# Order and tiles of the two halves of the first mixer: gated linear attention ahead of the recurrence

## The chip, the cores and the metric

The kernel runs on one core of one Trainium2 chip. The metric is the device time of one execution in microseconds (us). The kernel before takes 2805.81 us, the median of three runs (2805.32 to 2807.16).

## What is computed

Two blocks of two layers each on x (512 tokens, width 1024). The change lies in the first mixer of the first block; everything behind it stays. Cut to what matters:

```python
def even_mixer(u, w_in, conv_w, conv_b, rg_wa, rg_ba, rg_wx, rg_bx, rg_lam,
               gla_w_up, gla_b_up, gla_norm_g, w_out):
    xr, yr, q, k, v, g, zl = split(u @ w_in, [512, 512, 256, 256, 512, 512, 16])
    # recurrent half
    x = causal_dwconv(xr, conv_w, conv_b)
    r, i = sigmoid(x @ rg_wa + rg_ba), sigmoid(x @ rg_wx + rg_bx)      # 8 blocks of 64
    log_a = 8 * r * log_sigmoid(rg_lam)
    h = scan(exp(log_a), sqrt(-expm1(2 * log_a)) * (i * x))            # h_t = a_t h_(t-1) + u_t
    rg_out = h * gelu(yr)
    # gated linear attention (GLA), 4 heads, chunks of 64 tokens
    log_alpha = log_sigmoid(zl @ gla_w_up + gla_b_up) / 16
    bcum = cumsum(log_alpha) within a chunk
    q_dec, k_dec, k_end = q*exp(bcum), k*exp(-bcum), k*exp(b_last - bcum)
    o = causal(q_dec k_dec^T) v + q_dec state;  state = decay * state + k_end^T v
    o = rms_norm(o, gla_norm_g) * silu(g)
    return concat([rg_out, o]) @ w_out
```

## The kernel before

**Layout.** Activations lie transposed, 128 features in the partitions and 512 tokens along the free axis, so a vector of 1024 features is 8 tiles of 128x512. `H` ("hidden") has 32 such tiles, `M` ("mixer_out") 8, `TMP` ("tmp") 2, and `B` is the 8 PSUM banks. The mixer's tiles in `H` are named by number on the lines that begin with `XR, YR, Q, K_, GG, VT` (L448 to L451). The names EB, QD, KD, KE and T1 of GLA lie on tiles 20 to 29, the same tiles as RT, IT and AT_ of the recurrence (20 to 31). So GLA's elementwise work can't begin before the recurrence is through with them; `gla_u` waits for `rg_scan` 3.

**Products.** Every weight product is in fp32 split in two parts: weights high and low, input high and low, three matmuls for each 128x128 block. A product of one output tile (`gemm`, L654 to L656) is 24 matmuls of 128x128 on 512 columns. `gemm_tok` makes v with the tokens in the partitions, in 4 panels of 24 matmuls (L715 to L717). `gemm_pair` makes two outputs, the second two k-tiles behind the first, so that inputs which are just being made can be taken in as they come (L697 to L699). Its `busy` (L625) are matmuls of constants whose result isn't used. `gemm_bank` hands out banks 1 and 0 in turn, and waits for the eviction of the product before last.

**Weights.** A stream of 512 KB panels is loaded by SyncE into a ring of 4. Most panels are weights: ScalarE (ACT) writes the high part (`high`, L2047), VectorE (DVE) the low part (`low`, L1296), into one of 3 places. The others ("ada") belong to the modulations: VectorE alone multiplies and sums them (`modulation`, L1305). Their order in the stream is fixed: v0, v1, ada, v2, ada, v3, yr0, ada, yr1, ada, yr2, yr3, ada, gg0, ada, gg1, gg2, ada, gg3, ada, and then each of the eight even_out panels with two ada panels behind it. VectorE frees the place in the ring. `prepare(ahead(key))` stands by hand at places of the ScalarE and VectorE programs: it makes the panels up to the second one behind `key`. `high` waits until the third panel back has been used.

**Order.** Each engine's program is written out by hand, in order, and an engine that waits holds up all behind it. The functions `even` of the three programs hold the mixer. Before the change:

- TensorE (PE): eight products at once (`gemm_eight`), zl, v0 to v3 with the gate matmuls of the recurrence (L818) ahead of v2 and v3, GLA's logits 0 (L824), yr0, logits 1, yr1, yr2, yr3, the transposes of k_end (L835), gg0, GLA's scores and k^T v (L844, L853), gg1, gg2, GLA's outputs 0 (L870, L877), gg3, outputs 1, the sums of `gla_norm` (L890), then the pair even_out 0 and 1 with the second `gla_norm` inside it, then even_out 2 to 7.
- VectorE: convolution (L1332), the recurrence (L1542 to L1555), GLA's decays (`softplus_neg`, L1562 to L1578), mask and state (L1586, L1594), gelu (L1599 to L1605), then GLA's norm and gates (L1611 to L1624). `input_low` (L1463) splits the eight results.
- ScalarE: sigmoids (L2203), exp and tanh (L2208, L2212), sqrt (L2217), the eviction of v (L2068), softplus of GLA (L2225 and L2081 to L2085), its exps (L2231, L2238), evictions of yr and gg (L2061), gelu's square and tanh, the GLA outputs (L2257, L2262), the roots (L2089, L2092) and `input_high` (L2072), which writes UHI, the tiles that the gg products read.

Where ScalarE needs a function that its active table doesn't hold, a table load stands ahead of it (ACT_TABLE_LOAD). `exp_ln_tables` loads one by hand, which holds both exp and ln.

## Time and profile before

| | before |
|---|---|
| median of three runs | 2805.81 us |
| the profiled execution | 2809.87 us |
| its span (first to last instruction) | 2808.4 us |
| mean granted TensorE clock | 0.993 |
| TensorE busy | 2694.2 us, 96% |
| VectorE busy | 1626.6 us, 58% |
| ScalarE busy | 1122.9 us, 40% |
| DMA | 336.42 MB, mean 120 GB/s |

A row of an engine's timeline has the start and the length in us, the engine, the line in the kernel, the operation, its tiles written and read, and how often it stands in a row; in brackets the idle time ahead of it and who ended it. Matmuls are pipelined, so the time from one start to the next is what one costs, not its length. A row of "waits" has who waited, for whom, and then the total in us, how often, and the longest. A row of "windows" has the stretch in us, and for each engine its busy time and its number of instructions, and behind them the granted clock (1.00 is 2.4 GHz, 0.50 is 1.2 GHz), the busy share of the DMA engines, and GB/s.

### The profile page before, as it was taken

Reading aid. Unit: us, or ns where it says so; the run is one execution under the profiler, and the core shown is the slowest. Engines: PE = TensorE matmul, PEld = TensorE weight load, DVE = VectorE, ACT = ScalarE, POOL = GpSimd, SP = SyncE. Lnnn points to the kernel's source line nnn. Section 1 sums busy time; section 2 is a strip of 40 time slices with the busy share of each in tenths; the row PEclk is TensorE's granted clock in tenths of the full one; section 3 lists DMA queues with packets and bytes.
Section 4 is the critical chain, followed back from the end, with each engine's and each line's share of the span. In section 5 each row is a group of like instructions: output and inputs, shape, how many; then the busy total and the mean of one; then the engine's idle time right before and its main releaser. Section 6 shows DMA issues by size and latency. Waiting matters only on the chain.

```text
span 2808.4 us, 41819 instructions
## 1 busy us (share of the span) xinstructions
PE 2694.2 (96%) x17268; PEld 2119.8 (75%) x17268; DVE 1626.6 (58%) x2919; ACT 1122.9 (40%) x1964; POOL 9.4 (0%) x21
## 2 busy tenths in 40 slices
PE   7899999999999999999998899999999988999998
PEld 6677888867666788886876667888878766788886
DVE  7678646573555874657456755443465577533334
ACT  3544324234555432423345653222334466422222
POOL 0000000000000000000000000000000000000000
PEclk9999999999999999999999999999999999999999
DMA  8344555532221365563330013444433200222322
GB/s 308 105 150 166 195 173 180 179 133 91 76 76 56 117 206 198 181 205 111 103 116 17 3 61 120 143 142 150 143 120 108 90 3 2 92 96 98 98 98 83
DMA packets 92094, 336.42 MB, mean 120 GB/s; under 512 B 10481, under 2 KB 10737, under 8 KB 91777
## 3 DMA queue, kind: packets, MB, share of 16 engines
q1 hardware_dynamic: 86656, 314.87, 33.8%
q10 hardware_dynamic: 3936, 14.64, 1.4%
q0 software_dynamic: 1312, 4.23, 0.5%
q8 instruction: 138, 2.26, 0.3%
q14 instruction: 52, 0.42, 0.0%
HBM read 331.57 MB, written 2.13 MB: 119 GB/s over the span
## 4 chain that ended last, share of the span: by engine, by line
PE 46%; DVE 3%; ACT 3%; issue 1%; DVEq 0%; ACTq 0%
PE bank L654 12%; PE bank L655 12%; PE bank L656 12%; PE bank L933 1%; ACT probs L2294 1%; PE bank L918 1%; PE bank L904 1%; PE bank L1018 1%; PE bank L697 0%; PE bank L698 0%; PE bank L699 0%; PE bank L991 0%; PE bank L1192 0%; PE bank L1124 0%; PE bank L1006 0%
## 5 line engine op out<-in xcount | busy, mean ns | idle before, releaser
L1296 DVE TENSOR_TENSOR weights_low<-weight_ring,weights_high 128x1024 fp32r<-128x1024 f32 x404 | 493.9, 1224 | 428.0 <-ACT weights_high L2047 427.9
L654 PE MATMUL bank<-in_high,weights_high 128*128 128x512 f32 x1816 | 718.2, 396 | 15.0 <-DVE weights_low L1296 9.9
L656 PE MATMUL bank<-in_high,weights_low 128*128 128x512 f32 x1816 | 708.2, 390 | 0.0
L655 PE MATMUL bank<-in_low,weights_high 128*128 128x512 f32 x1816 | 708.0, 390 | 0.0
L2047 ACT ACTIVATE weights_high<-weight_ring 128x1024 fp32r<-128x1024 f32 x404 | 424.5, 1051 | 432.2 <-PE bank L656 301.4
L654 PEld LDWEIGHTS bank<-in_high,weights_high 128*128 128x128 f32 x1816 | 341.6, 188 | 100.1 <-issue 17.8
L655 PEld LDWEIGHTS bank<-in_low,weights_high 128*128 128x128 f32 x1816 | 341.8, 188 | 72.4 <-issue 3.1
L656 PEld LDWEIGHTS bank<-in_high,weights_low 128*128 128x128 f32 x1816 | 341.4, 188 | 72.0
L654 PE MATMUL bank<-hidden_split,weights_high 128*128 128x512 f32 x864 | 336.9, 390 | 0.0
L656 PE MATMUL bank<-hidden_split,weights_low 128*128 128x512 f32 x864 | 336.1, 389 | 0.0
L655 PE MATMUL bank<-hidden_split,weights_high 128*128 128x512 f32 x864 | 336.1, 389 | 0.0
L1305 DVE CUSTOM_DVE_ANT_0 weight_ring<-weight_ring,silu_c,vectors 128x1024 f32<-128x1024 f32 x192 | 244.2, 1278 | 0.1
L655 PEld LDWEIGHTS bank<-hidden_split,weights_high 128*128 128x128 f32 x864 | 162.2, 188 | 34.1 <-issue 0.5
L654 PEld LDWEIGHTS bank<-hidden_split,weights_high 128*128 128x128 f32 x864 | 162.2, 188 | 34.1 <-issue 0.5
L656 PEld LDWEIGHTS bank<-hidden_split,weights_low 128*128 128x128 f32 x864 | 162.2, 188 | 33.8
L2162 ACT ACTIVATE hidden_split<-tmp 128x512 fp32r<-128x512 f32 x108 | 68.3, 632 | 269.3 <-DVE tmp L1836 200.7
L2061 ACT ACTIVATE tmp<-bank 128x512 f32<-128x512 f32 x76 | 45.4, 597 | 228.7 <-PE bank L656 225.1
L1468 DVE TENSOR_TENSOR hidden_split<-tmp,hidden_split 128x512 fp32r<-128x512 f32 x108 | 74.8, 692 | 75.4 <-ACT hidden_split L2162 75.4
L1357 DVE SCALAR_TENSOR_TENSOR residual<-bank,modulations,residual 128x512 f32<-128x512 f32 x64 | 48.0, 750 | 118.7 <-PE bank L656 118.7
L2294 ACT ACTIVATE probs<-probs,columns 128x256 f32<-128x256 f32 (+4 forms) x144 | 73.7, 514 | 101.8 <-DVE columns L1641 100.0
L1836 DVE TENSOR_TENSOR tmp<-bank,tmp 128x512 f32<-128x512 f32 x44 | 30.4, 691 | 113.6 <-PE bank L656 113.6
L2061 ACT ACTIVATE tmp<-bank,vectors 128x512 f32<-128x512 f32 (+1 forms) x65 | 44.6, 687 | 129.0 <-PE bank L656 125.8
(394 smaller groups left out, 3377.6 us busy)
## 6 DMA issues: line engine op xcount, KB each, us to landing
weight_ring<-stream SPq DMA_DIRECT2D x596, 512.0 KB, 3.4
mixer_out<-cmp ACTq DMA_DIRECT2D x6, 1024.0 KB, 4.9
hidden<-forget_rows POOLq DMA_DIRECT2D x16, 256.0 KB, 3.6
residual<-x ACTq DMA_DIRECT2D x4, 512.0 KB, 8.4
mixer_out<-cmp SPq DMA_DIRECT2D x2, 1024.0 KB, 6.3
out<-mixer_out ACTq DMA_DIRECT2D x4, 512.0 KB, 3.0
constants<-consts ACTq DMA_DIRECT2D x1, 1821.5 KB, 9.9
silu_c<-c ACTq DMA_DIRECT2D x2, 512.0 KB, 4.4
```

Source lines behind the costliest of these rows:

```text
L654: pe.matmul(bank[:, :], WHI[:, z, cols], high, start=(k == 0), stop=False)
L655: pe.matmul(bank[:, :], WHI[:, z, cols], low, start=False, stop=False)
L656: ins = pe.matmul(bank[:, :], WLO[:, z, cols], high, start=False, stop=(k == ktiles - 1))
L1296: v.tensor_tensor(WLO[:, z, :], ring[:, n % RING, :], WHI[:, z, :].bitcast(F32), ALU.subtract).then_inc(*mark("weights_low", "low", n))
L1305: v.tensor_tensor_reduce(w, w, SC[:, :], 1.0, vec1("ada_b", col, col + 1), ALU.mult, ALU.add, MODS[:, col:col + 1]).then_inc(*mark("modula ...
L1357: v.scalar_tensor_tensor(X[:, m, :], B_of(key)[:, :], gcol_[:, m:m + 1], X[:, m, :], ALU.mult, ALU.add).then_inc(*mark("residual", "evicte ...
L1468: v.tensor_tensor(HSPLIT[:, 1, at_, :], tmp, HSPLIT[:, 0, at_, :].bitcast(F32), ALU.subtract).then_inc(*mark("vector_mlp", *event))
L1836: v.tensor_tensor(tmp, B_of(("gup", l, j))[:, :], tmp, ALU.mult).then_inc(*mark("vector_mlp", "evicted", ("gup", l, j)))
L2047: s.activation(WHI[:, i % NSPLIT, :], ring[:, n % RING, :], ACT.Copy).then_inc(*mark("weights_high", "high", n))
L2061: s.activation(dst, view(B_of(key)[:, :]), func, **kw).then_inc(*mark("scalar_evict", "evicted", key))
L2162: s.activation(HSPLIT[:, 0, at_, :], tmp, ACT.Copy).then_inc(*mark("scalar_mlp", *event))
L2294: s.activation(p, p, ACT.Exp, bias=nm, scale=-1.0, accum_out=COL[:, c + 2 + z:c + 3 + z]).then_inc(*mark(sem, *name, "exp", i))
```

## The change

It reorders the first mixer and moves tiles; no product and no elementwise operation on data is left out, and the stream of weights keeps its order.

- **Tiles.** GLA's softplus and k_dec go to TMP, its cumulated decays to M 6 and 7, a temporary to M 4 and 5, EB to H 14 and 15; q_dec and k_end are written over q and k. None of them lies on a tile of the recurrence any more. The recurrence's own temporary leaves M 4 to 7 for RT.
- **Order.** The logits go ahead of v1; softplus and decays go ahead of the recurrence, between and around its sigmoids. The transposes of k_end go behind v3, scores and k^T v behind yr0, then yr1, yr2, yr3. The four gg products now stand behind the parts of GLA that make its output: outputs 0, gg0, outputs 1, gg1, norm 0, gg2, norm 1, gg3.
- **Split.** The four recurrent results of the mixer are split into other tiles (H 4 to 7, where yr was, and H 0 to 3), not into UHI and ULO, which the gg products still read. The pair of even_out has no `busy` and no norm inside it.
- **Tables.** With the new order ScalarE's functions alternate more often between tables.

```diff
     XR, YR, Q, K_, GG, VT = 0, 4, 8, 10, 12, 16
     RT, IT, AT_ = 20, 24, 28
-    EB, QD, KD, KE, T1, KET = 20, 22, 24, 26, 28, 30
-    OG = [Q, Q + 1, K_, K_ + 1]
+    KET, EB = 12, 14
+    OG = [K_, K_ + 1, Q, Q + 1]
+    gla_x = lambda m: TMP[:, m, 0:T]
+    gla_cum = lambda m: M[:, 6 + m, :]
+    gla_t = lambda m: M[:, 4 + m, :]
+    MIX_LO = (2, 3, 0, 1)
+    even_split = lambda k: (HSPLIT[:, 0, YR + k, :], HSPLIT[:, 0, MIX_LO[k], :]) if k < 4 else u_split(k)
...
@@ TensorE, even()
+                elif i == 1:
+                    for m in range(2):
+                        pe.wait_ge(*at("evicted", ("q", m)))
+                        pe.wait_ge(*at("evicted", ("zl",)))
+                        ins = pe.matmul(B[2 + m][:, :], vec1("gla_up", m * P, m * P + P, rows=16), ZL, start=True, stop=True)
+                        ins.then_inc(*mark("tensor_even", "gla_logits", m))
...
             gemm_tok(("v",), 4, 2, 512, ("v",), B[4:8], gates)
+            pe.wait_ge(*at("loads"))
             for m in range(2):
-                pe.wait_ge(*at("rg_gate", 1, 3))
...
-                gemm(("yr", m), u_split)
-            gemm(("yr", 2), u_split)
-            gemm(("yr", 3), u_split)
-            for m in range(2):
+                pe.wait_ge(*at("rg_gate", 1, 3 * m))
                 pe.wait_ge(*at("gla_ke", m))
...
-            gemm(("gg", 0), u_split)
+            gemm(("yr", 0), u_split)
+            pe.wait_ge(*at("v_out", NTB - 1))
             pe.wait_ge(*at("ket", 1))
...
-            gemm(("gg", 1), u_split)
-            gemm(("gg", 2), u_split)
+            for m in range(1, 4):
+                gemm(("yr", m), u_split)
...
             pe.wait_ge(*at("gla_state"))
             gla_out(0)
+            gemm(("gg", 0), u_split)
+            gla_out(1)
+            gemm(("gg", 1), u_split)
+            gla_norm(0)
+            gemm(("gg", 2), u_split)
+            gla_norm(1)
             gemm(("gg", 3), u_split)
-            gla_out(1)
-            gla_norm(0)
...
-        gemm_pair([("even_out", 0), ("even_out", 1)], u_split, lambda k: ("even_low", k),
-                  lambda k: gla_norm(1) if k == 3 else None)
-        project(lambda m: ("even_out", m), 0, None, 2)
+        gemm_pair([("even_out", 0), ("even_out", 1)], even_split, lambda k: ("even_low", k), idle=0)
+        project(lambda m: ("even_out", m), 0, None, 2, even_split)
@@ VectorE, even()
...
+            for m in range(2):
+                softplus_neg(sem, gla_x(m), gla_x(m), gla_cum(m), ("gla", m))
+            for m in range(2):
+                v.tensor_scalar(gla_x(m), gla_x(m), -1.0 / 16.0, None, ALU.mult).then_inc(*step(sem))
+                v.wait_ge(*last(sem))
+                v.tensor_tensor_scan(gla_cum(m), const("chunk_reset"), gla_x(m), 0.0, ALU.mult, ALU.add).then_inc(
+                    *mark(sem, "gla_cum", m))
+            prepare(ahead(("v", 2)))
+            for m in range(2):
+                qd, k_, kd, bc, eb, t1 = H[:, Q + m, :], H[:, K_ + m, :], gla_x(m), gla_cum(m), H[:, EB + m, :], gla_t(m)
+                v.wait_ge(*at("gla_exp", m))
+                v.tensor_tensor(qd, qd, eb, ALU.mult).then_inc(*step(sem))
+                v.tensor_tensor(kd, k_, t1, ALU.mult).then_inc(*step(sem))
...
+                v.tensor_tensor(t3, bc3[:, :, GLA_CH - 1:GLA_CH].broadcast_to([P, 8, GLA_CH]), bc3,
+                                ALU.subtract).then_inc(*mark(sem, "gla_end", m))
+            for m in range(2):
+                k_ = H[:, K_ + m, :]
+                v.wait_ge(*at("gla_end_exp", m))
+                v.tensor_tensor(k_, k_, gla_t(m), ALU.mult).then_inc(*mark(sem, "gla_ke", m))
+            prepare(ahead(("v", 3)))
...
             v.tensor_tensor(i_, i_, xr, ALU.mult).then_inc(*step(sem))
...
             v.wait_ge(*at("rg_decay"))
...
+            v.tensor_tensor(xr, a, a, ALU.mult).then_inc(*step(sem))
...
+            v.scalar_tensor_tensor(r, xr, 1.0, r, ALU.add, ALU.mult).then_inc(*mark(sem, "rg_ratio"))
+            prepare(ahead(("yr", 0)))
+            v.wait_ge(*at("rg_ratio"))
+            v.memset(H[:, XR:XR + 2, :], 0.0).then_inc(*step(sem))
             v.wait_ge(*at("rg_sqrt"))
...
+            v.tensor_tensor(i_, i_, r, ALU.mult).then_inc(*mark(sem, "rg_in"))
...
             for m in range(4):
+                if m == 2:
+                    prepare(ahead(("yr", 1)))
                 v.tensor_tensor_scan(M[:, m, :], H[:, AT_ + m, :], H[:, IT + m, :], 0.0, ALU.mult, ALU.add).then_inc(
                     *mark(sem, "rg_scan", m))
...
+            prepare(ahead(("yr", 2)))
...
+            prepare(ahead(("yr", 3)))
...
+            prepare(ahead(("gg", 0)))
...
+            def mix_low(k):
+                high, lo = even_split(k)
+                v.wait_ge(*at("even_high", k))
+                v.tensor_tensor(lo, M[:, k, :], high.bitcast(F32), ALU.subtract).then_inc(*mark(sem, "even_low", k))
...
+                v.wait_ge(*at("evicted", ("gg", h)))
...
+            gla_sum(0)
+            v.wait_ge(*at("yr_tanh"))
+            v.scalar_tensor_tensor(th, th, 1.0, yr, ALU.add, ALU.mult).then_inc(*step(sem))
+            v.wait_ge(*last(sem))
+            v.scalar_tensor_tensor(rgo, th, 0.5, rgo, ALU.mult, ALU.mult).then_inc(*mark(sem, "rg_mix"))
+            prepare(ahead(("gg", 1)))
+            mix_low(0)
+            mix_low(1)
+            gla_sum(1)
+            mix_low(2)
+            mix_low(3)
+            prepare(ahead(("gg", 2)))
+            gla_mix(0)
+            gla_mix(1)
+            gla_mix(2)
+            prepare(ahead(("gg", 3)))
+            mix_low(4)
+            gla_mix(3)
+            for h in range(1, 4):
+                mix_low(4 + h)
@@ ScalarE, even()
...
             evict(("zl",), ZL, view=lambda z: z[0:16, :])
+            s.wait_ge(*at("loads"))
+            s.wait_ge(*at("xr_conv", 1))
             prepare(ahead(("v", 1)))
...
+            for m in range(2):
+                s.wait_ge(*at("gla_logits", m))
+                s.activation(gla_x(m), B[2 + m][:, :], ACT.Identity, bias=vec1("gla_b", m, m + 1)).then_inc(*mark(sem, "gla_u", m))
+            for m in range(2):
+                s.wait_ge(*at("gla_u", m))
+                softplus(sem, gla_x(m), gla_cum(m), ("gla", m))
...
+            gate(0)
+            prepare(ahead(("v", 2)))
+            for m in range(2):
+                s.wait_ge(*at("gla_cum", m))
+                s.activation(H[:, EB + m, :], gla_cum(m), ACT.Exp).then_inc(*step(sem))
+                s.activation(gla_t(m), gla_cum(m), ACT.Exp, scale=-1.0).then_inc(*mark(sem, "gla_exp", m))
+            for m in range(2):
+                s.wait_ge(*at("gla_end", m))
+                s.activation(gla_t(m), gla_t(m), ACT.Exp).then_inc(*mark(sem, "gla_end_exp", m))
+            prepare(ahead(("v", 3)))
+            gate(1)
...
             for m in range(4):
...
             for m in range(4):
...
+                ins = s.activation(H[:, RT + m, :], H[:, RT + m, :], ACT.Tanh, scale=LS[:, m:m + 1])
...
             for m in range(2):
                 s.wait_ge(*at("ke_turned", m))
...
+                s.activation(ket[:, :, m * P:m * P + P], r4(B[2 + m][:, :]), ACT.Copy).then_inc(*mark(sem, "ket", m))
+            prepare(ahead(("yr", 0)))
+            s.wait_ge(*at("rg_ratio"))
+            s.activation(wide(RT), wide(RT), ACT.Sqrt, scale=-1.0).then_inc(*mark(sem, "rg_sqrt"))
+            for m in range(4):
+                evict(("yr", m), H[:, YR + m, :])
+            th = M[:, 4:8, :].rearrange("p a t -> p (a t)")
+            s.wait_ge(*at("gla_ke", 1))
             s.wait_ge(*at("evicted", ("yr", 3)))
...
             s.activation(th, wide(YR), ACT.Square).then_inc(*mark(sem, "yr_square"))
...
+            prepare(ahead(("gg", 0)))
             intra(0)
+            s.wait_ge(*at("yr_poly"))
+            s.activation(th, th, ACT.Tanh, scale=float(np.sqrt(2.0 / np.pi))).then_inc(*mark(sem, "yr_tanh"))
             square(0)
+            evict(("gg", 0), H[:, GG, :], ACT.Silu)
+            prepare(ahead(("gg", 1)))
+            mix_high(0, ("rg_mix",))
+            mix_high(1, ("rg_mix",))
+            intra(1)
+            mix_high(2, ("rg_mix",))
+            mix_high(3, ("rg_mix",))
+            s.wait_ge(*at("gla_state"))
+            evict(("gg", 1), H[:, GG + 1, :], ACT.Silu)
+            square(1)
+            prepare(ahead(("gg", 2)))
+            exp_ln_tables()
+            for h in range(4):
+                root(h)
+            evict(("gg", 2), H[:, GG + 2, :], ACT.Silu)
             evict(("gg", 3), H[:, GG + 3, :], ACT.Silu)
...
+            for h in range(4):
+                mix_high(4 + h, ("gla_mix", h))
             exp_ln_tables()
```

Of the hunks of VectorE and ScalarE only the new order is shown; the order that it replaces is that of the functions printed above. `gate(half)` is the loop over `rg_gate`, `mix_high` is `input_high` with the new place for its result, and `root`, `square` and `intra` are as before.

## Rows read from the trace of the kernel before

**Rows 1.** The page, part 1: busy time, share of the span, instructions.

```profile
PE 2694.2 (96%) x17268; PEld 2119.8 (75%) x17268; DVE 1626.6 (58%) x2919; ACT 1122.9 (40%) x1964; POOL 9.4 (0%) x21
```

**Rows 2.** The waits of TensorE between 60 and 230 us.

```profile
PE bank L654 <- DVE weights_low L1296: 8.7, 4, 7.6
PE bank L835 <- DVE hidden L1578: 2.7, 1, 2.7
PE bank L890 <- ACT hidden L2262: 2.3, 1, 2.3
...
PE bank L697 <- DVE in_low L1463: 1.6, 3, 0.9
```

**Rows 3.** The waits of ScalarE between 60 and 230 us, the first.

```profile
ACT weights_high L2047 <- DMA weight_ring<-stream: 28.3, 8, 5.7
```

**Rows 4.** The timeline of TensorE, from the first v panel to even_out 2 and 3.

```profile
68.50 0.39 PE L715 MATMUL bank<-weights_high,in_high 128*128 128x512 f32 x1
...
79.38 3.59 PE L818 MATMUL bank<-hidden 128*128 128x512 f32 x8
...
97.24 1.12 PE L824 MATMUL bank<-probs_T,vectors 16*128 16x512 f32 x2
...
119.00 0.76 PE L654 MATMUL bank<-in_high,weights_high 128*128 128x512 f32 x1 [7.55 <-DVE weights_low L1296]
119.56 0.63 PE L655 MATMUL bank<-in_low,weights_high 128*128 128x512 f32 x1
...
122.12 0.40 PE L655 MATMUL bank<-in_low,weights_high 128*128 128x512 f32 x1
...
134.90 0.66 PE L835 MATMUL bank<-constants,hidden 128*128 128x128 f32 x4 [2.66 <-DVE hidden L1578]
...
142.54 1.39 PE L844 MATMUL bank<-hidden 64*64 64x64 f32 x58
...
168.43 3.39 PE L625 MATMUL bank<-constants 128*128 128x384 f32 x10
...
178.06 1.99 PE L890 MATMUL bank<-hidden,constants 128*128 128x512 f32 x4 [2.30 <-ACT hidden L2262]
...
189.82 0.47 PE L654 MATMUL bank<-in_high,weights_high 128*128 128x512 f32 x1
...
195.83 0.47 PE L654 MATMUL bank<-in_high,weights_high 128*128 128x512 f32 x1 [0.30 <-DVE weights_low L1296]
```

**Rows 5.** Two windows of 4 us, around the longest wait and around a wait of 2.30 us.

```profile
116.00:120.00 4.00, 1.00 (x3) 0.84 (x4) 3.56 (x6) 3.90 (x7) 0.00 (x0) 0.50 0.32 91
...
176.00:180.00 4.00, 1.94 (x5) 0.99 (x6) 2.76 (x4) 3.94 (x7) 0.00 (x0) 1.00 0.00 0
```

**Rows 6.** The timeline of ScalarE, 92 to 176 us.

```profile
92.60 1.28 ACT L2208 ACT_TABLE_LOAD   x1
93.89 2.56 ACT L2208 ACTIVATE hidden<-hidden,columns 128x512 f32<-128x512 f32 x4
...
103.30 1.92 ACT L2217 ACTIVATE mixer_out<-mixer_out 128x2048 f32<-128x2048 f32 x1 [1.19 <-DVE mixer_out L1549]
105.12 2.04 ACT L2068 ACTIVATE hidden<-bank 128x512 f32<-128x512 f32 x4
...
175.69 0.71 ACT L2089 ACTIVATE hidden<-bank,constants 128x512 f32<-128x512 f32 x1
```

**Rows 7.** The timeline of VectorE, 92 to 153 us.

```profile
92.61 2.29 DVE L1542 TENSOR_TENSOR hidden<-hidden 128x2048 f32<-128x2048 f32 x1 [13.14 <-ACT hidden L2203]
...
107.85 4.57 DVE L1555 TENSOR_TENSOR_SCAN mixer_out<-hidden 128x512 f32<-128x512 f32 x4
...
116.42 1.28 DVE L1305 CUSTOM_DVE_ANT_0 weight_ring<-weight_ring,silu_c,vectors 128x1024 f32<-128x1024 f32 x1
...
117.63 1.22 DVE L1296 TENSOR_TENSOR weights_low<-weight_ring,weights_high 128x1024 fp32r<-128x1024 f32 x1
...
148.80 4.46 DVE L1594 SCALAR_TENSOR_TENSOR hidden<-hidden,bank 128x128 f32<-128x128 f32 x14
```

More of the change, by code:

```diff
@@ L776, in layer_norm, with project @@
             ins.then_inc(*mark("tensor_means", "ln_var", i))
-        def project(key, i, ready, first=0):
+        def project(key, i, ready, first=0, x=u_split):
             for m in range(first, KT):
@@ L783, in project @@
                 else:
-                    gemm(key(m), u_split, ready=ready if m == 0 else None)
+                    gemm(key(m), x, ready=ready if m == 0 else None)
                 if i and m == 4:
@@ L2216, in even @@
-            s.wait_ge(*at("rg_ratio"))
-            s.activation(th, th, ACT.Sqrt, scale=-1.0).then_inc(*mark(sem, "rg_sqrt"))
             evict_blocks(("v",), ("v", 3), B[4:8], lambda b: vt[:, b, :], 512, ("v_out",))
-            exp_ln_tables()
-            s.wait_ge(*at("loads"))
-            for m in range(2):
-                x = H[:, QD + m, :]
-                s.wait_ge(*at("gla_logits", m))
-                s.wait_ge(*at("rg_scan", 3))
-                s.activation(x, B[2 + m][:, :], ACT.Identity, bias=vec1("gla_b", m, m + 1)).then_inc(*mark(sem, "gla_u", m))
-                s.wait_ge(*last(sem))
-                softplus(sem, x, H[:, KE + m, :], ("gla", m))
-                evict(("yr", m), H[:, YR + m, :])
```

126 lines of the change are left out of this document (25 added, 101 removed).

## The prediction, made before the changed kernel ran

> **What bounds the kernel now.** I read the busy times first: TensorE works 96% of the span [rows 1], so a gain has to be a wait of TensorE that goes, and there are few. Its waits between 60 and 230 us come next [rows 2], then its timeline, which gives the places [rows 4]. All of the change lies between the first v panel (68.50 us) and the start of even_out 2 (189.82 us): 121.3 us. Four things in it are not matmuls that the result needs:
> - Waits. Of the 8.7 us for weights_low, 7.55 stand ahead of yr2 at 119.00; 0.30 (at 195.83) and one more like it lie behind the stage, which leaves 8.0 inside. 2.7 are for GLA's k_end at 134.90, 2.3 for the ScalarE square of GLA's output at 178.06, 1.6 for input splits in the pair. Together 14.6 us. The reader should see that 7.55 us are not really for weights. VectorE and ScalarE come to yr2's panel late, since softplus of GLA had to wait for the scans (107.85 plus 4.57 [rows 7]), whose tiles it overwrites.
> - The unused matmuls at 168.43: 3.4 us.
> - A slow clock behind the long waits. From 119.56 to 122.12 six steps take 0.427 us each; at the full clock 48 matmuls from 68.50 to 79.38 take 0.227 each. The window around it was granted 0.50, the lower of the two levels (1.2 of 2.4 GHz) [rows 5]. About 7 steps here and 8 behind the wait at 134.90 (the rows there look the same) cost 0.2 us each: 3.1 us.
> All three make 21.1 us, so 100.2 us are work. No matmul is added, none that is used is removed.
>
> **The change: the early part.** I follow the three engines with durations from the rows. One gemm is 24 x 0.227 = 5.44 us, 5.5 with the switch between kinds of matmuls. The chain on TensorE: v0 68.5 to 73.9; both logits 2.2 (1.12 each [rows 4]); v1 to 81.6; gates 3.5 (79.38, x8 in 3.59); v2 to 90.6; gates to 94.0; v3 to 99.5; transposes 1.0; yr0 to 106.1. Then it waits for ket 1.
>
> ScalarE: the logits are there at 75.2 and 76.3, the softplus steps (two additions of bias, then six dependent steps at 0.64 and a little [rows 6]) are done at 80.9, and it loads the sigmoid table in time for the gates, which TensorE paces to 85.8. From here ScalarE is the chain: weights high 1.0, table 1.3, two exps to 89.3; VectorE does six 512-wide products for both halves (about 0.65 each, a quarter of the 2.29 of a wide one plus its start [rows 7]) to 93.3; exp of the end 0.6, high of yr1 1.0, table 1.3, four sigmoids 2.4: 98.7. Table 1.3, eight exps and tanhs 5.0 (2.56 for four [rows 6]): 104.9. Eviction of v 2.0 (105.12 [rows 6]), ket 1.2: **108.1**. TensorE had been ready at 106.1: a new wait of 2.1 us, and behind ScalarE's queue lie yr evictions that nobody needs yet. The added waits for the constants and for `xr_conv` 1 cost nothing: the second convolution ends near 68.3, before ScalarE gets there.
>
> **The recurrence, now behind GLA.** VectorE: i*x after the gates at 98.7, then a*a after the decays (102.4) and the ratio, 2.25 us each [rows 7]: 107.3. An ada panel and yr2's low part (1.28 and 1.22 [rows 7], the low waits for ScalarE's high at 109.1): 110.4. Sqrt on ScalarE, 1.3 table and 1.9 [rows 6]: 112.3. Product 2.3, four scans 4.6, yr3's low 1.1, ada and gg0's low 2.5: 122.9. Mask and clearing about 1.6 (an estimate from the two short operations on 512 columns), state 4.5 (148.80 [rows 7]): **128.9**. TensorE: scores and k^T v 3.3 (1.39 for the scores [rows 4], the rest about 1.9), to 111.5, then three yr to 128.1. A new wait of 0.8 us for the state.
>
> **GLA's output behind the gg products.** TensorE goes from 129.0: outputs 2.0 each, norms 1.8 each (178.06 [rows 4]), four gg 22.6: it is done with gg3 at 159.3. Each of the steps between finds its partner early: outputs 1 needs the eviction of outputs 0 (132.6, TensorE comes at 136.7); norm 0 needs the square (138.1, comes at 144.4), with gelu's tanh ahead of it on ScalarE; norm 1 needs the second square (147.6, comes at 151.8). So the 2.3 us wait goes, and so do those for the splits of the pair: the recurrent quarter of the mixer's output is split by 148 us. What is late next: ScalarE's roots 2 and 3 (two steps of about 0.65 each, 0.71 for the first [rows 6]) end at 155.3, the silu table 1.3 and gg2 0.5 make 157.1, VectorE's product needs that, and behind the product stand two ada panels and the low part of even_out 1: 0.7 + 2.5 + 1.2 = 161.5. The pair asks for both low parts at its start. A new wait of **2.3 us** (161.6 against 159.3). The pair then takes 11 us without another wait, for the last splits (163 to 165 us) are there before its fifth k-tile at 165.7.
>
> **The sum.** Stage before 121.3 us, after 100.2 + 2.1 + 0.8 + 2.3 = 105.4: 15.9 us less, taken as 16. The placing above, step by step, ends the pair at 172.8 and gives 17.0; I take the smaller, since a placing leaves small starts out. Behind the pair nothing changes. The weight stream there is tight: ScalarE waited 28.3 us for panels [rows 3]. But TensorE hardly waited for it (0.30, twice), and the panels of even_out 2 are made at 169 while TensorE wants them at 172.8, where before they came in the same moment. So that part keeps its length or gives 0.7 us. Against its own time the changed kernel's span would be 2808.4 - 16 = 2792.4. The profiled execution took 2809.87, 4.1 above the median, so I take 16 from the median: 2805.81 - 16 = **2789.8 us**.
>
> **The tables.** Table loads in the mixer rise from 6 to 9 or 10 (whether tanh and silu share one after the sqrt no row shows; it stands where ScalarE has time). A load costs 1.28 us, and the exp behind it starts 0.01 us after its end (92.60, 93.89 [rows 6]). Three of them are in the chain to ket and one is in the chain to the pair; they are counted above. The Trainium skill speaks against this order (ScalarE: Activation LUTs, "Rules for kernel authors": do all functions of one table before switching), and "What ACT_TABLE_LOAD costs" gives 1283 ns for the load and about 1380 ns more for a drain. By that page the four loads on the two chains would add some 5.5 us. The trace agrees with the load and not with the drain: the load at 92.60 follows the sigmoids without a gap.
>
> **The rivals.**
> 1. *ScalarE's chains are longer than I sum them.* The mechanism: six alternations between the tables and three hand-overs to VectorE stand ahead of ket, and each can add its start. The pure sum has nothing for it. Were each of the four loads to hold its engine for twice its row, 4 x 1.3 = 5.2 us come back: 2795.0. For it: each of these steps starts only when the one before is done, and a queue that holds copies of weights between them has no way around. Against it: the load at 92.60 and the exps at 93.89 follow on each other without a hole [rows 6]. The page's drain would come out here too, at 2789.8 + 5.5 = 2795.3. Chance 0.15.
> 2. *The clock falls in the new waits.* Behind the wait at 134.90 (2.66 us) eight matmuls ran slow, behind the wait of 2.30 us at 178.06 none (granted 1.00 there [rows 5]). The new waits of 2.1 and 2.3 us lie by the second, and no unused matmuls cover the one ahead of the pair. Two falls cost 2 x 1.6 = 3.2 us: 2793.0. Chance 0.15.
> 3. *The weight stream gives the gain back.* The pair starts 17 us sooner, and the places of the ring come free by VectorE. Were each of the six gemms behind it to wait 0.33 us, as two did before: 2 us back, 2791.8. The six gemms need 18 panels in 33 us; the stream moved at that pace before. Chance 0.05.
> 4. *Slower: the clock stays low.* If the new order starves TensorE in short waits all through the stage, matmuls run at 0.427 and not 0.227. It decides from the point where more than 80 additional matmuls (16 us by 0.2) run slow, a quarter of the stage's 336; with all from the ket wait on (nine gemms, 216 matmuls) it costs 43 us: 2833. Against it: in every stretch with long products the clock was back after 4 us. Chance 0.03.
> 5. *Nothing comes of it,* as VectorE is the true bound: it would need 16 more us of waits for low parts. VectorE is busy 58% of the span [rows 1], none of its operations is added, and in my placing each low part is there before TensorE asks for it, but for even_out 1. Chance 0.04, at 2805.
>
> **How the numbers follow.** The forecast has 0.58: its own range is 2787 to 2792.5 (16 us with 17 and the 0.7 of the stream at the low end, a short wait or two at the high end). Its range, rivals 1, 2 and 3 together hold about 0.93, of which 2786 to 2798 keeps eight in ten and a little; the low end allows for new waits that don't come (all 5.2 gone would be 2784.6), the high end for rivals 1 and 2 together. A measurement of this kernel can tell about 0.2% (5.6 us) from no change. All but rivals 4 and 5 are beyond that: faster 0.93, the same 0.04, slower 0.03.
>
> **What would show it.** In the profile after: no wait of TensorE near 7 us ahead of yr2; in its place one of about 2 us ahead of the scores with ket as releaser, one under 1 us ahead of the first outputs, one of 2 to 3 us ahead of the pair for weights_low. Even_out 2 starts near 173 us. The granted clock is 1.00 in the whole stage. Wrong would be: waits in the yr or gg gemms for weights_low (my VectorE queue is then too short), a start of even_out 2 beyond 178 us (rival 1), steps of 0.427 (rival 2), or a distance from even_out 2 to the end of the span that isn't the 2618.6 us of before within 1 us (rival 3).

## The result and the profile after

The changed kernel takes 2789.45 us (median of four runs, 2787.22 to 2789.91), the kernel before 2806.48 us (four runs, 2805.32 to 2809.57): a ratio of 0.9936, with a 95% interval of 0.9919 to 0.9953. That is 17.0 us less, where 16 were forecast. The profiled execution took 2789.05 us.

Busy times first (page, part 1, with the line that gives the span), against [rows 1]:

```profile
span 2787.6 us, 41806 instructions
...
PE 2685.7 (96%) x17258; PEld 2120.1 (76%) x17258; DVE 1626.7 (58%) x2919; ACT 1127.6 (40%) x1968; POOL 9.4 (0%) x21
```

VectorE works as long as before, ScalarE 4.7 us longer and with four more instructions, which are four more table loads. TensorE is busy 8.5 us less, of which 3.4 are the ten unused matmuls that went; the other 12.3 us of the 20.8 between the two profiled spans are its idle time, so its waits come next. These are those between 60 and 215 us (total, times, longest), against [rows 2]:

```profile
PE bank L702 <- DVE weights_low L1299: 2.9, 1, 2.9
PE bank L845 <- ACT hidden L2257: 2.2, 1, 2.2
PE bank L659 <- ACT hidden L2218: 1.7, 1, 1.7
PE bank L756 <- ACT mixer_out L2152: 1.4, 1, 1.4
```

The 7.55 us ahead of yr2, the 2.66 for k_end and the 2.30 for the square are gone. Two waits have come in: ahead of the scores for ket (L2257), and ahead of the pair for even_out 1's low part (L1299). The third lies at 61.60, ahead of the stage, and the fourth at the layer norm, behind it; the kernel before has both. The timeline of TensorE gives the places, against [rows 4]:

```profile
67.17 0.39 PE L720 MATMUL bank<-weights_high,in_high 128*128 128x512 f32 x1
...
97.97 1.03 PE L836 MATMUL bank<-constants,hidden 128*128 128x128 f32 x8
...
106.62 1.61 PE L845 MATMUL bank<-hidden,tmp 64*64 64x64 f32 x56 [2.17 <-ACT hidden L2257]
...
111.48 0.50 PE L659 MATMUL bank<-in_high,weights_high 128*128 128x512 f32 x1
...
128.02 1.16 PE L870 MATMUL bank<-hidden 64*64 64x64 f32 x64
...
160.78 0.47 PE L702 MATMUL bank<-hidden_split,weights_high 128*128 128x512 f32 x1 [2.89 <-DVE weights_low L1299]
...
162.38 0.63 PE L702 MATMUL bank<-hidden_split,weights_high 128*128 128x512 f32 x1
162.81 0.63 PE L703 MATMUL bank<-hidden_split,weights_high 128*128 128x512 f32 x1
...
173.38 0.39 PE L659 MATMUL bank<-hidden_split,weights_high 128*128 128x512 f32 x1
```

The stage runs from the first v panel at 67.17 to even_out 2 at 173.38: 106.2 us, where it took 121.3. From 106.62 to yr1 at 111.48 the scores and k^T v take 4.86 us, and 3.24 before. Behind the second wait the steps are 0.43 us apart, nearly twice the full rate's 0.227. Two windows tell why (length, then busy time with counts of PE, PEld, DVE, ACT and POOL, the granted clock, the DMA share, GB/s):

```profile
108.00:112.00 4.00, 4.00 (x84) 3.79 (x77) 2.92 (x3) 3.99 (x4) 0.00 (x0) 0.64 0.82 257
...
160.00:164.00 4.00, 3.22 (x10) 2.65 (x11) 3.90 (x7) 1.44 (x3) 0.00 (x0) 0.76 0.88 271
```

Behind both waits the clock fell for some microseconds to the lower of its two levels, 1.2 GHz. Each fall cost 1.6 us here (1.4 to 1.7 in the profiles below): 4.86 against 3.24, and 12.60 for the pair against the 10.96 to 11.01 that it took in five profiles below where its clock stayed at 1.00.

**Where the 20.8 us between the two profiled spans are.** Ahead of the stage 1.3. In it 15.1. From even_out 2 to the first layer-norm matmul 1.75 (35.25 to 33.50 us). Next to it 0.2, and in the second block, whose code is the same, 2.4 (1509.26 to 1506.84 us). That last stretch ran between 1506.8 and 1510.2 us in the other profiles, so the 2.4 are scatter between executions. Stage and even_out make 16.85, near the 17.0 of the medians. The agreement is closer than one profile can promise: the repeat below has a stage 1.5 us shorter, as one of the two falls didn't come.

### The profile page after: what moved, and what is told of

The parts are those of the page before. It is cut to its first block, busy times and chain, and to the rows that moved or that the text cites. A ratio compares the mean times of both kernels' runs of the same rounds, so it can differ in the third digit from the quotient of the medians.

```text
span 2787.6 us, 41806 instructions
## 1 busy us (share of the span) xinstructions
PE 2685.7 (96%) x17258; PEld 2120.1 (76%) x17258; DVE 1626.7 (58%) x2919; ACT 1127.6 (40%) x1968; POOL 9.4 (0%) x21
## 4 chain that ended last, share of the span: by engine, by line
PE 46%; ACT 4%; DVE 3%; issue 1%; DVEq 0%; ACTq 0%
PE bank L659 12%; PE bank L661 12%; PE bank L660 12%; ACT probs L2325 1%; PE bank L937 1%; PE bank L922 1%; PE bank L1022 1%; PE bank L908 1%; PE bank L702 0%; PE bank L703 0%; PE bank L704 0%; PE bank L1196 0%; PE bank L995 0%; PE bank L1010 0%; PE bank L1206 0%
## 5 line engine op out<-in xcount | busy, mean ns | idle before, releaser
L1299 DVE TENSOR_TENSOR weights_low<-weight_ring,weights_high 128x1024 fp32r<-128x1024 f32 x404 | 493.8, 1223 | 417.2 <-ACT weights_high L2069 417.1
L659 PE MATMUL bank<-in_high,weights_high 128*128 128x512 f32 x1792 | 708.1, 395 | 6.0 <-DVE in_low L1448 3.1
L661 PE MATMUL bank<-in_high,weights_low 128*128 128x512 f32 x1792 | 698.0, 390 | 0.0
L660 PE MATMUL bank<-in_low,weights_high 128*128 128x512 f32 x1792 | 698.0, 389 | 0.0
L659 PE MATMUL bank<-hidden_split,weights_high 128*128 128x512 f32 x888 | 346.4, 390 | 0.0
L660 PE MATMUL bank<-hidden_split,weights_high 128*128 128x512 f32 x888 | 345.6, 389 | 0.0
L661 PE MATMUL bank<-hidden_split,weights_low 128*128 128x512 f32 x888 | 345.6, 389 | 0.0
L660 PEld LDWEIGHTS bank<-hidden_split,weights_high 128*128 128x128 f32 x888 | 166.7, 188 | 35.1 <-issue 0.5
L659 PEld LDWEIGHTS bank<-hidden_split,weights_high 128*128 128x128 f32 x888 | 166.7, 188 | 34.9 <-issue 0.5
```

The source lines that it names most:

```text
L659: pe.matmul(bank[:, :], WHI[:, z, cols], high, start=(k == 0), stop=False)
L660: pe.matmul(bank[:, :], WHI[:, z, cols], low, start=False, stop=False)
L661: ins = pe.matmul(bank[:, :], WLO[:, z, cols], high, start=False, stop=(k == ktiles - 1))
L1299: v.tensor_tensor(WLO[:, z, :], ring[:, n % RING, :], WHI[:, z, :].bitcast(F32), ALU.subtract).then_inc(*mark("weights_low", "low", n))
```

## The experiments

Every diff is against the changed kernel. I read each profile by the same distances: "the stage" is the first v panel to even_out 2, "even_out" is even_out 2 to the first layer-norm matmul. Where no number of runs is given, the time is that of one execution, and what counts is its profile.

**Does a table load cost more than its row?** One more load goes into ScalarE's chain to ket.

```diff
 def even():            # ScalarE, behind the loop over rg_tanh
+            exp_ln_tables()
             evict_blocks(("v",) ...
```

> The changed kernel with one more table load (1.28 us) on ScalarE, between the last tanh of the recurrence and the eviction of v. If ScalarE's queue sets the wait ahead of the scores, as I hold, that wait grows from 2.17 to 3.45 us and the start of the scores moves by 1.28 us. The start of the first GLA outputs moves by 1.3 us with it, for yr1 to yr3 follow without a break. If a table load also held the engine for a drain of 1.38 us, as the Trainium skill has it (ScalarE: Activation LUTs, What ACT_TABLE_LOAD costs), the wait would grow by 2.66 us. If VectorE or the transposes set the wait, it stays at 2.17 us.

Measured: 2793.59 us. The wait ahead of the scores grew from 2.17 to 3.64 us, by 1.47. The first two rows are ScalarE's timeline, the third is TensorE's:

```profile
103.82 1.28 ACT L2098 ACT_TABLE_LOAD   x1
105.11 2.07 ACT L2090 ACTIVATE hidden<-bank 128x512 f32<-128x512 f32 x4
...
108.30 1.39 PE L845 MATMUL bank<-hidden,tmp 64*64 64x64 f32 x58 [3.64 <-ACT hidden L2258]
```

The load takes 1.28 and the eviction behind it starts 0.01 us after its end. ScalarE's chain is what TensorE waits for, and a load costs its row and 0.2 us more. Of these 0.12 are an overlap that it ends: the last tanh has a length of 0.71 us, the eviction starts 0.61 behind its start in the changed kernel, and the load here 0.73 behind it. Rival 1's doubled loads would have made the growth 2.6 us, and the drain that the Trainium skill states (ScalarE: Activation LUTs, "What ACT_TABLE_LOAD costs") 2.66.

**Can the ket wait be hidden behind yr1?**

```diff
             gemm(("yr", 0), u_split)
+            gemm(("yr", 1), u_split)
             ...
-            for m in range(1, 4):
+            for m in range(2, 4):
```

> The changed kernel with TensorE's yr1 ahead of the scores and k^T v instead of behind them. The wait for ket 2.17 us goes, as yr1 fills it, and with it the slow clock in the scores (1.6 us). My theory: the first outputs then wait for the GLA state, whose chain over ScalarE and VectorE (ready near 127.0 us after the span's start) doesn't move: TensorE comes 3.8 us sooner, at 124.2, and waits about 2.8 us. So the first outputs start only 1.0 us sooner (127.0). Rival: the state hangs on TensorE (k^T v), then all 3.8 us are gained.

Measured: 2790.25 us. The wait ahead of the scores is gone and the scores run at full clock, but the state, which needs k^T v, now comes late:

```profile
127.69 0.52 PE L871 MATMUL bank<-hidden 64*64 64x64 f32 x20 [2.84 <-DVE hidden L1600]
```

From v0 to the first outputs it is 59.93 us, where it was 60.85: 0.9 less, of 3.8 (2.17 of wait, 1.6 of slow clock) that went at the scores. The wait moved from one hand-over to the next. The clock didn't fall behind the 2.84 us. A wait of 2.17 us is worth only what the next one leaves of it.

**Is the pair's wait the order of VectorE's queue?** The low part of even_out 1's panel goes ahead of the third product of GLA's mix, and its high part ahead of the last two roots.

```diff
             gla_mix(1)
-            gla_mix(2)
             prepare(ahead(("gg", 3)))          # VectorE: low part
+            gla_mix(2)
...
-            for h in range(4):
-                root(h)
+            root(0)
+            root(1)
+            prepare(ahead(("gg", 3)))          # ScalarE: high part
+            root(2)
+            root(3)
```

> The changed kernel with the panel of even_out 1 (ScalarE: behind the second root; VectorE: its two ada panels and the low part behind the second of GLA's last products) made before, not after, the third product, which waits for the silu table. If VectorE's queue behind that product sets the wait of 2.89 us ahead of the pair, as I hold, the low part is there at 157.5 and the wait falls under 1 us (the eviction of gg3 is what is left, 0.7); the slow clock behind it (8 steps, 1.6 us) may go with it: even_out 2 starts 2.2 to 3.8 us sooner, if no split in the pair comes late. Rival: the stream's panel is not there before 156 us, then the wait stays over 2 us.

Measured: 2784.43 us, a stage of 101.6 us. The low part starts at 154.74 and not at 159.31. By the distance from v0 that is 4.7 us earlier; 1.4 of them are this execution's scores, which ran at full clock and let the queue come sooner, and in the timed repeat, whose scores were slow, it is 3.3. What is left of the wait ends with gg3's eviction, which the second bank of the pair needs:

```profile
154.74 1.22 DVE L1299 TENSOR_TENSOR weights_low<-weight_ring,weights_high 128x1024 fp32r<-128x1024 f32 x1
...
157.92 0.47 PE L702 MATMUL bank<-hidden_split,weights_high 128*128 128x512 f32 x1 [0.73 <-ACT hidden L2083]
```

Of the 4.6 us in the stage 2.2 are the wait (2.89 to 0.73) and 3.2 the two falls of the clock that this execution didn't have, less 0.64 for a wait for the state, which shows now that the scores are faster. Its timed repeat stands below.

**Is it the wait, or the idle array, that lowers the clock?** Both waits are filled with matmuls whose result is not used.

```diff
             gemm(("yr", 0), u_split)
+            busy(B[(len(turns) + 1) % 2], 3)
...
-        gemm_pair([("even_out", 0), ("even_out", 1)], even_split, lambda k: ("even_low", k), idle=0)
+        gemm_pair([("even_out", 0), ("even_out", 1)], even_split, lambda k: ("even_low", k), idle=4)
```

> The changed kernel with unused matmuls in its two waits: 3 ahead of the scores (0.68 us each), 4 ahead of the pair. It tells what the clock costs. If the waits alone let it fall, the granted clock is 1.00 in scores and pair: scores and k^T v take 3.24 us instead of 4.86, the pair 11.0 instead of 12.6, the waits shrink by what the fillers take, and even_out 2 starts up to 3.2 us sooner (less 0.6 where the GLA state is then late). If the slow stretches come from something else (the kind of matmul, the DMA), both stay as they are and nothing is gained.

Measured: 2787.69 us, a stage of 103.55. The window of the scores is granted 1.00 where it was 0.64, and the pair takes 11.00 us. TensorE at the scores:

```profile
108.07 1.39 PE L846 MATMUL bank<-hidden,tmp 64*64 64x64 f32 x58 [0.23 <-ACT hidden L2258]
```

and the window around it:

```profile
108.00:112.00 4.00, 3.93 (x131) 3.70 (x132) 2.70 (x4) 3.97 (x3) 0.00 (x0) 1.00 0.51 161
```

The stage is 2.7 us shorter than in the profile of the changed kernel, of 3.2 for two falls; TensorE comes to the first outputs sooner and waits 0.62 us for the state there. The scores and the pair start as soon behind their releasers as without the fillers. Whether it was the fillers that kept the clock up, one profile can't show: without them it stayed up behind the ket wait in two profiles of eight and ahead of the pair in two of five (counted below), so that both would stay up by chance in about one of ten (an estimate).

**What is the late part of the change worth?** GLA's output and the gg panels go back to the old order, with the early part as changed.

```diff
+            for m in range(3):
+                gemm(("gg", m), u_split)
             gla_out(0)                         # behind the wait for the state
-            gemm(("gg", 0), u_split)
+            gemm(("gg", 3), u_split)
             gla_out(1)
-            gemm(("gg", 1), u_split)
             gla_norm(0)
-            gemm(("gg", 2), u_split)
-            gla_norm(1)
-            gemm(("gg", 3), u_split)
...
# gla_norm(1) at the pair's fourth k-tile; VectorE and ScalarE late as before
```

> The changed kernel with its late part as before: gg0 to gg2 ahead of the first outputs, gg3 between the outputs, the first norm behind them, the second inside the pair with its unused matmuls, and the recurrent quarter split into the tiles that the gg products read, behind gg3. The early part (GLA's own tiles, logits and decays ahead of the recurrence) stays. It splits the 15.1 us of the stage. From the first outputs to even_out 2 the kernel before took 32.9 us; the same is expected here (waits of 2.3 and about 1.6 us and 3.4 us of unused matmuls). Yr3 ends where it did, three gg make 16.4 us, so even_out 2 starts 48 to 50 us after the end of yr3 against 45.4 in the changed kernel: the late part is worth 3 to 4.5 us, the early part 10.5 to 12. Rival: the late part holds most of it, since GLA's results are now early enough anyway; then even_out 2 starts over 8 us later.

Measured: 2804.63 us, and the stage is 117.3 us. But this is my order and not the old one: gg3's low part stands behind the recurrent product, which waits for the gelu.

```profile
146.15 2.29 DVE L1630 SCALAR_TENSOR_TENSOR mixer_out<-mixer_out,hidden 128x2048 f32<-128x2048 f32 x1 [11.42 <-ACT mixer_out L2286]
...
154.45 0.76 PE L659 MATMUL bank<-in_high,weights_high 128*128 128x512 f32 x1 [8.74 <-DVE weights_low L1298]
```

So it says nothing of the late part, but shows what one misplaced panel costs: 8.74 us of wait, and a slow clock in the product behind it. With that low part ahead of the wait for the tanhs of yr (one line more: `prepare(ahead(("gg", 1)))` ahead of `v.wait_ge(*at("yr_tanh"))`):

> As late_part_undone, but VectorE makes gg3's low part ahead of gelu's last products, not behind them. In that run TensorE waited 8.7 us for it and then ran slow for a few us; VectorE itself had waited 11.4 us for gelu's tanh, which stands behind gg2's eviction on ScalarE. Expected: this wait is gone, and what is left is the late part as the kernel before had it. The stage from the first v panel to even_out 2 takes 107 to 109.5 us, against 104.7 to 106.2 in the changed kernel and 117.3 in the run before this one. So the late part is worth 2 to 4 us and the early part 12 to 14 of the stage's 15 to 16.6. Rival: another wait of over 4 us takes its place, then the late order does not go with the early one, and the two parts can't be priced apart.

Measured: 2798.19 us, a stage of 108.8 us, even_out 34.7. TensorE's waits there again include the square (total, times, longest):

```profile
PE bank L892 <- ACT hidden L2273: 2.3, 1, 2.3
...
PE bank L702 <- DVE in_low L1619: 1.8, 3, 1.0
```

The scores' clock didn't fall here, and at the pair 3.4 us of unused matmuls ran; the wait of 2.3 us had no fall behind it. So the early part gives 121.3 - 108.8 = 12.5 us, and the late part 2.6 us in the stage against the profile of the changed kernel, 4.1 against its repeat below, and 1.2 in even_out. The late figure hangs on the clock: the two profiles of the changed kernel hold two falls and one, this one none; with the falls taken off (and 0.64 for the state put on) the changed stage is 103.6, and the late part gives about 5 us. Of the early part's 12.5 some 3 are the slow clock behind the two old waits. Each share is from one profile.

**Is it the place of the recurrent half's split?** It goes back behind gg3, in the old tiles, and nothing else changes.

```diff
-    even_split = lambda k: (HSPLIT[...], ...) if k < 4 else u_split(k)
+    even_split = lambda k: u_split(k)
...
# mix_high(0..3) behind gg3's eviction, mix_low(0..3) behind the low part of even_out 1
```

> The changed kernel with one piece of its late part undone: the four recurrent results are split into the tiles that the gg products read, so they wait for gg3, as before. ScalarE has then eight copies and VectorE eight low parts behind gg3 instead of four. The wait ahead of the pair is set by even_out 1's low part (VectorE near 160.5 us), ScalarE's first copies are done by then, and TensorE takes a k-tile in 0.7 to 1.4 us while VectorE makes a low part in 0.65. Expected: the pair starts within 0.7 us of where it did, and small waits of 0.5 to 2 us in all arise at the fifth to eighth k-tile, for the GLA parts come four copies later. So the other place is worth 1 to 2.5 us. Rival: it is worth nothing (under 0.3 us), the panel hides it.

Measured: 2791.59 us, a stage of 106.43 against 106.21. The pair waits for the low part of its first input in place of the weights, which end 0.6 us ahead of it:

```profile
PE bank L702 <- DVE in_low L1620: 3.2, 1, 3.2
```

That is 3.2 us where it was 2.9, with a slow clock behind both waits in both profiles: in this order the split elsewhere is worth 0.2 to 0.3 us, and the expectation's rival, which had it under 0.3, was right. The pair's wait ends with several things at nearly one time.

**Can all waits go by one order?** The scores behind yr1, the first gg panel ahead of the state, gg2 and gg3 evicted ahead of the roots.

```diff
             gemm(("yr", 1), u_split)           # ahead of the scores
...
+            gemm(("gg", 0), u_split)
             gla_out(0)                         # behind the wait for the state
-            gemm(("gg", 0), u_split)
-            gla_out(1)
             gemm(("gg", 1), u_split)
+            gla_out(1)
             gla_norm(0)
             gemm(("gg", 2), u_split)
-            gla_norm(1)
             gemm(("gg", 3), u_split)
+            gla_norm(1)
# ScalarE: gg2 and gg3 evicted, then root(0), root(1), and root(2 + h) with the splits
```

> A version that should beat both, from what the first four runs showed: yr1 ahead of the scores, gg0 ahead of the first outputs (so that TensorE has work until the GLA state is there), gg2 and gg3 both ahead of the second norm, so that their silu needs no table load behind the roots and the panel of even_out 1 is made before the roots. One table load less. TensorE's waits for ket (2.2 us), for the state (2.8 us in the run with yr1 ahead of the scores) and for the pair's panel (2.9 us) should all go; the fifth to eighth k-tile of the pair may wait 1 to 2 us in all for the last roots. From the first v panel to even_out 2: 99 to 101 us against 106.2 in the changed kernel, 101.6 with the panel first and 121.3 before. The total is 5 to 7 us below the changed kernel. Rival: GLA's outputs now come later than the gg products can cover, and the pair waits over 4 us for its last k-tiles: no gain over the run with the panel first.

Measured: 2787.39 us (four runs, 2785.29 to 2789.52), ratio 0.9925 (0.9909 to 0.9941). Two table loads less, no wait ahead of scores, state or norms, and a stage of 100.6 us, in the pair of which 1.95 us are waits for splits. The stage has 5.6 us less than in the changed kernel; the kernel, 2 us, and not the 5 to 7 that I had expected. To see whether that holds, the changed kernel was timed again on the same chip, and gates ahead and the version with the panel first together on another, each beside the kernel before. The last column is the distance from the first v panel to the last layer norm of the first block; it was 1213.59 us in the first profile of the changed kernel and 1210.78 in the first of gates ahead.

> The changed kernel as it is, on the chip of the other three. It tells what repeats. The waits of 2.2 and 2.9 us stand where they were, within 0.2 us. Theory on the clock: whether it falls behind such a wait is chance (in the five profiles of the changed order it fell behind two of three waits over 2.1 us ahead of the scores and behind two of three ahead of the pair), so the stage from the first v panel to even_out 2 takes 103 to 106.2 us. Behind the mixer the time from one execution to the next varies by 2 us or more with nothing changed there. The total is 15 to 19 us below before. Rival: the slow stretches belong to the code, then both are there again and the stage takes 106.2 within 0.3.

> The kernel of pair_panel_first, timed. Against the changed kernel (2789.5 us on two chips) it should be 3 to 5 us faster: 2784 to 2787 us, a ratio to the kernel before near 0.992. Trace: stage from the first v panel to even_out 2 101 to 103 us, even_out 33.5 us. Rival: its single time of 2784.4 was a lucky execution, and the median is not below 2788.

> The kernel of gates_ahead, timed again on the same chip as panel_first_timed. Its stage was 1.0 us shorter (100.6 us) and its even_out 0.8 us longer, so by the trace the two should be the same within 1 us, and within what a measurement can tell. Rival: its median stays 2 us over the other's, then something behind the mixer depends on the order.

| | median us | runs | ratio (95%) | below the kernel before on its chip | stage | even_out | to the last layer norm |
|---|---|---|---|---|---|---|---|
| changed kernel again | 2789.65 | 4 | 0.9931 (0.9913 to 0.9948) | 19.6 | 104.67 | 33.50 | 1211.86 |
| panel first | 2786.12 | 4 | 0.9922 (0.9908 to 0.9935) | 21.2 | 102.46 | 33.50 | 1209.70 |
| gates ahead | 2790.54 | 5 | 0.9935 (0.9922 to 0.9949) | 16.8 | 100.64 | 33.91 | 1213.68 |

The shortest stage doesn't make the fastest kernel. On one chip gates ahead takes 4.4 us more than panel first (2787.19 to 2791.51 against 2785.51 to 2786.43); against the changed kernel it was 2.3 us faster on the chip that both ran on, and the last column puts the two level. The second profile of gates ahead shows where the gain is given back: behind even_out 7, at the layer norm, ScalarE waits for a panel that hasn't landed, VectorE's low part waits for ScalarE's high part, the residual stands behind it, and TensorE waits 2.08 us.

```profile
202.88 1.06 ACT L2068 ACTIVATE weights_high<-weight_ring 128x1024 fp32r<-128x1024 f32 x1 [2.18 <-DMA weight_ring<-stream]
...
203.97 1.23 DVE L1300 TENSOR_TENSOR weights_low<-weight_ring,weights_high 128x1024 fp32r<-128x1024 f32 x1 [1.99 <-ACT weights_high L2068]
...
205.85 1.12 PE L752 MATMUL bank<-residual,constants 128*128 128x512 f32 x2 [2.08 <-DVE residual L1355]
```

In the windows of 40 us its clock there is 0.91:

```profile
200.00:240.00 40.00, 35.05 (x113) 21.63 (x112) 27.14 (x42) 18.48 (x28) 0.00 (x0) 0.91 0.26 87
```

The same window in the changed kernel is granted 1.00:

```profile
200.00:240.00 40.00, 37.14 (x136) 24.89 (x135) 30.57 (x49) 20.61 (x30) 0.00 (x0) 1.00 0.36 122
```

From the layer norm to the next marker both profiles of gates ahead take longer (371.6 and 368.4 us) than the changed kernel (366.3). In the 371.6 the wait of 2.08 us and a slow clock that lost some 3.4 us (0.91 over 40 us) make up the 5.3 us; in the 368.4 there is a wait of 0.24 us and a shorter fall. From even_out 2 to the layer norm ScalarE waits 25.6 us for panels of the stream, 22.3 in the changed kernel: what TensorE saves ahead of it meets weights that haven't landed. That one panel was late is shown; that the shorter stage is why, and the stream the last cause, is argued from these waits, and a faster stream wasn't tried.

Panel first is the best version in these runs: its median is 3.3 to 3.5 us below those of the changed kernel, which were not taken on its chip, and 21.2 below the kernel before on its own. Set against the kernel before each time, it gains 1.6 to 4.2 us on the changed kernel. The intervals of the ratios overlap; the shorter wait in both of its profiles is what speaks for it.

## Why the prediction was right, point by point

The time was right to 0.4 us and its sign too. The sum under it was right in part, and its errors cancelled, so that a hit within 0.4 us is luck:

| | forecast us | profile after |
|---|---|---|
| work of the stage | 100.2 | 97.9 |
| wait for ket | 2.1 | 2.17 |
| wait for the state | 0.8 | 0 |
| wait ahead of the pair | 2.3 | 2.89 |
| slow clock | 0 | 3.2 |
| stage | 105.4 | 106.2 |
| even_out gives | 0 to 0.7 | 1.75 |

- **The early part** held. The chain over three engines was placed to end ket 39.6 us behind v0, and it ended 39.3 behind it. The wait of 7.55 us went, and no low part came late in its place. Undoing only the late part left 12.5 us of the gain, so most of it is here.
- **The state** was forecast ready 60.4 us behind v0 and came after 59.9. TensorE came at 60.85, as its slow scores had delayed it. In the two profiles of this order whose scores ran at full clock the wait was 0.64 and 0.62 us, near the 0.8. The term was right and its cover came by accident.
- **The pair's wait** was named with its cause (the roots, the silu table, the product, two ada panels, the low part), and the profile shows that chain. VectorE's queue ahead of the pair:

```profile
156.29 0.69 DVE L1629 TENSOR_TENSOR mixer_out<-hidden 128x512 f32<-128x512 f32 x1 [1.96 <-ACT hidden L2083]
156.90 1.28 DVE L1308 CUSTOM_DVE_ANT_0 weight_ring<-weight_ring,silu_c,vectors 128x1024 f32<-128x1024 f32 x1
158.10 1.28 DVE L1308 CUSTOM_DVE_ANT_0 weight_ring<-weight_ring,silu_c,vectors 128x1024 f32<-128x1024 f32 x1
159.31 1.22 DVE L1299 TENSOR_TENSOR weights_low<-weight_ring,weights_high 128x1024 fp32r<-128x1024 f32 x1
```

  Moving that low part ahead of the third product took 2.2 of the 2.9 us away, in both profiles.
- **The work** was mis-sized by 2.3 us. I took for it everything of the old stage that was no wait, no unused matmul and no slow step, and that residue held starts behind the old waits, which went with them. The pair shows it best: with its waits and the norm inside it taken off, it took 12.7 us before, in four pieces, and 11.0 after, in one. The placing, whose work comes to 99.1 us, was nearer, and I had chosen the smaller gain.
- **The clock** is the step that failed. I forecast 1.00 in the whole stage and gave two falls 0.15, from one wait of 2.30 us behind which the clock had stayed [rows 5]. One row could not say that it always does. Of eight profiles with the ket wait (2.16 to 3.64 us) the scores were slow in six; of five with a pair wait of 2.73 to 3.21 us the pair was slow in three; where the wait at these two places was under 1.2 us or filled, in none. Other places say the same of chance: behind the waits of 2.84 us for the state and 2.3 for the square there was no fall, and at the layer norm, where every profile has a wait of 1.44 us, it fell in four of the twelve profiles with the early part changed. Rival 2 did happen, at its price of 2 x 1.6 us, and the mis-sized work hid it in the sum.
- **Even_out** gave more than I allowed: 1.75 us. The four restarts for panels that came late (two with waits of 0.30 [rows 4] and 0.36) went, with their starts. The distance from even_out 2 to the end is 2614.2 us, not 2618.6 within 1: 1.75 are these, 0.2 lie next to them and 2.4 are the scatter of the second block. That test of mine was too narrow for one execution.
- **Rival 1** and the drain fall. The tables are loaded ten times, the upper of my two counts, and ket was not late. In ScalarE's timeline of the changed kernel:

```profile
84.41 1.05 ACT L2069 ACTIVATE weights_high<-weight_ring 128x1024 fp32r<-128x1024 f32 x1
85.48 1.28 ACT L2240 ACT_TABLE_LOAD   x1
86.77 0.63 ACT L2240 ACTIVATE hidden<-mixer_out 128x512 f32<-128x512 f32 x1
```

  The load starts 0.02 us behind the copy, and the exp 0.01 us behind the load. The Trainium skill (ScalarE: Activation LUTs, "What ACT_TABLE_LOAD costs") adds about 1380 ns of drain to 1283 ns of load. These rows bear out the second number and not the first, and the added load's 1.47 us agrees with them.
- **Rival 3,** the weight stream, took nothing at a gain of 17 us (even_out got shorter). At a larger one it showed: gates ahead lost most of what its stage had won, in even_out and at the layer norm, and in one of its two profiles a late panel ended the wait there.
- **Rivals 4 and 5** did not come: the clock was low for a few microseconds each time, and VectorE's low parts were there.

## What to carry to other kernels

A wait of 7 us that a trace puts down to weights can be an order: one engine's queue stood behind another chain whose tiles it was to overwrite, and tiles of its own with another order took it away without one needed instruction less on the busy engines. After such a change look for what stands between the last small step and the first large one: moving a 1.2 us panel ahead of a product that wasn't urgent took another 2.2 us of wait away, and spared the risk of a slow clock behind it (1.6 us). And time a stage's gain to the end of the kernel, since a stage that got 4 to 5.6 us shorter here gave the kernel 2 us in one comparison and nothing in the next.

## What the runs showed of the hardware

- Behind the same wait (2.2 us ahead of the scores, 2.9 ahead of the pair) the clock falls to 1.2 GHz in some executions and stays at 2.4 GHz in others, at the same place of the same code: the changed kernel's pair took 12.60 us in one profile and 11.01 in the other. A fall costs 1.4 to 1.7 us. With matmuls without a use in both waits it stayed at 1.00, in the one profile that was taken.
- A table load is 1.28 us and is followed at once, on a ScalarE that works before and after it; in a chain that TensorE waits for it cost 1.47 us.
- A stretch whose code is untouched (the second block, some 1508 us) differs by 3.4 us between executions, so that a difference of two single profiles is no measure of a gain of that size.
